# Last stage of a hybrid decoder step: small token tile first, every second sum on TensorE, four result buffers

## The reference, cut to what matters

```python
top_w, top_i = lax.top_k(pf, TOP_K)                                    # TOP_K = 2
top_w = top_w / jnp.sum(top_w, axis=-1, keepdims=True) * p_sel[:, None]
...
act = jax.nn.silu(gate) * up * combine_w[:, sl, None]
out = out + jnp.einsum('nef,efd->nd', act, w_ed[sl])
...
x = x + _hier_moe(_rmsnorm(x, norm_ffn_w), w_rc, w_rf, w_eu, w_ed)
...
y_prompt = _rmsnorm(xp, norm_final_w)     # y = x * rsqrt(mean(x*x) + 1e-6) * w
y_sample = _rmsnorm(xs, norm_final_w)
```

## Time and profile before

| | us |
|---|---|
| median of 3 runs (lowest to highest) | 1739.56 (1738.46 to 1739.89) |
| the profiled execution, own time | 1737.92 |
| its span in the profile | 1736.2 |
| PE busy, whole span | 1519.3 (88%) |
| DVE busy, whole span | 700.4 (40%) |
| ACT busy, whole span | 397.1 (23%) |
| POOL busy, whole span | 222.0 (13%) |

### The profile page before, as it was taken

How to read it: one execution, slowest core, us unless ns; L and a number is a source line. 1 busy time by engine, 2 the same in 40 slices (tenths; PEclk the granted TensorE clock), 3 DMA queues, 4 the chain that set the end, 5 groups by cost and what they waited for, 6 DMA issues and landing times. The chain is left out here.

```text
span 1736.2 us, 16020 instructions
## 1 busy us (share of the span) xinstructions
PE 1519.3 (88%) x6054; PEld 947.5 (55%) x6054; DVE 700.4 (40%) x1086; ACT 397.1 (23%) x639; POOL 222.0 (13%) x224
## 2 busy tenths in 40 slices
PE   8889999989998989699999599999807999999970
PEld 6556666645655656356989366555403444444430
DVE  4378676023243322885785333221241111111118
ACT  4111101015565563131211500011101111111113
POOL 0000010000000000254287000000041000000004
PEclk9998999999999999799899899999958999999995
DMA  5261148411100113324101722111127999999938
GB/s 160 72 101 49 50 131 240 116 50 40 38 27 26 38 26 89 92 62 139 57 1 29 298 75 75 62 60 64 43 73 302 377 367 373 370 368 367 368 144 292
DMA packets 191315, 247.83 MB, mean 143 GB/s; under 512 B 62548, under 2 KB 125432, under 8 KB 190976
## 3 DMA queue, kind: packets, MB, share of 16 engines
q1 hardware_dynamic: 165508, 186.79, 33.7%
q10 hardware_dynamic: 18140, 34.48, 5.1%
q0 software_dynamic: 7584, 25.44, 3.9%
HBM read 188.86 MB, written 57.82 MB: 142 GB/s over the span
## 5 line engine op out<-in xcount | busy, mean ns | idle before, releaser
L654 PE MATMUL P<-arena 128*128 128x352 f32 (+1 forms) x1728 | 547.0, 473 | 5.2 <-ACT arena L1791 5.2
L654 PEld LDWEIGHTS P<-arena 128*128 128x128 f32 (+1 forms) x1728 | 329.4, 194 | 193.1 <-issue 37.4
L1083 PE MATMUL P<-arena 128*128 128x512 f32 x512 | 227.8, 598 | 0.8 <-ACT arena L2060 0.8
L1083 PEld LDWEIGHTS P<-arena 128*128 128x128 f32 x512 | 95.8, 192 | 110.0 <-issue 110.0
L1031 PE MATMUL P<-arena 128*128 128x512 f32 (+1 forms) x288 | 126.8, 594 | 1.9 <-DVEq L1532 1.9
L999 PE MATMUL P<-arena 128*128 128x352 f32 x384 | 115.4, 464 | 10.1 <-DVE arena L1518 10.1
L1070 PE MATMUL P<-arena 128*128 128x512 f32 x256 | 115.3, 593 | 0.9 <-DVE arena L1661 0.9
L1641 DVE COPY arena<-P 128x512 f32<-128x512 f32 x32 | 22.1, 692 | 213.7 <-PE P L1057 213.7
L999 PEld LDWEIGHTS P<-arena 128*128 128x128 f32 x384 | 73.7, 192 | 52.0 <-issue 12.1
L1031 PEld LDWEIGHTS P<-arena 128*128 128x128 f32 (+1 forms) x288 | 50.9, 181 | 66.7 <-issue 64.2
L579 POOL TENSOR_TENSOR arena<-arena,N 64x256 f32<-64x256 f32 x96 | 80.0, 833 | 49.7 <-ACT arena L1994 26.9
(11 more groups left out here) (384 smaller groups left out, 1842.4 us busy)
## 6 DMA issues: line engine op xcount, KB each, us to landing
arena<-in_w_expert_up_dram SPq DMA_DIRECT2D x32, 2048.0 KB, 12.2
arena<-in_w_expert_down_dram SPq DMA_DIRECT2D x32, 1024.0 KB, 8.2
arena<-in_w_in_dram SPq DMA_DIRECT2D x36, 512.0 KB, 3.8
y_d<-arena ACTq DMA_DIRECT2D x32, 512.0 KB, 7.7
gate_d<-arena ACTq DMA_DIRECT2D x16, 528.0 KB, 4.1
arena<-gate_d SPq DMA_DIRECT2D x16, 528.0 KB, 4.5
arena<-in_x_prompt_dram SPq DMA_DIRECT2D x16, 512.0 KB, 4.3
y_d<-zero SPq DMA_DIRECT2D x1, 8192.0 KB, 33.2
```

Of the source, the lines that this page charges most:

```text
L654: m = pe.matmul(P[0:p, b + j, 0:TBK], w[:, k, 0:p], hT[:, k, TBK * j:TBK * j + TBK], start=f, stop=l)
L1083: m = pe.matmul(P[:, i % 2, :], xgT[i % 2][:, k, :], WU[i % NWE][:, k, :], start=k == 0, stop=k == KD - 1)
```

## The change

The order of the token tiles in the tail becomes `ORDER` = tile 8 (32 rows), then 0, 1, ..., 7; p counts the place in this order. At odd p (tiles 0, 2, 4, 6) PE makes the sum in two banks of PSUM of its own: `x1` through `ident`, then the two gathered tiles through diagonal matrices `DG` of the weights, six `pe.matmul` of 512 columns a tile, of which the two of `x1` stand ahead of the wait for the gathers. At even p (tiles 8, 1, 3, 5, 7) DVE sums as before. DVE scales all nine tiles; its order becomes C0, N0, C2, N1, N2, C4, N3, N4, C6, N5, N6, C8, N7, N8. There are four `yout` buffers and four store semaphores (two of them reused). The eight `DG` matrices are built by DVE while it works on expert tile 6.

```diff
-        yout = [at(q + 6432 + i * D, D) for i in range(2)]
+        yout = [at(q + 4384 + i * D, D) for i in range(4)]
+        DG = h2T[0]
...
+        s_out4 = s_yst + [s_wo, s_wf]
+        STORED = (0, 0, 16, 16)
...
+        ORDER = [TT_ - 1] + list(range(TT_ - 1))
+
+        def summed_by_pe(p):
+            return p % 2 == 1
+
+        def bank_sum(p):
+            return P[:, 2 * (p // 2):2 * (p // 2) + 2, :]
...
 @block.gpsimd
-            for i in range(TT_):
+            for p, i in enumerate(ORDER):
                 n = rows(i)
-                if i >= 3:
-                    pool.wait_ge(s_acc, i - 2)
+                if p >= 3 and summed_by_pe(p - 3):
+                    pool.wait_ge(s_job, N_JOBS + (p - 3) // 2 + 1)
+                elif p >= 3:
+                    pool.wait_ge(s_acc, (p - 3) // 2 + 1)
                 for j in range(2):
                     pool.indirect_dma_start(yg[2 * i + j][0:n], None, y_d,
                                             bass.IndirectOffsetOnAxis(pos_i[0:n, j, i:i + 1], 0)
-                                            ).then_inc(s_yg[i % 3], 16)
+                                            ).then_inc(s_yg[p % 3], 16)
...
 @block.tensor
                 down(hi - 1)
+                pe.wait_ge(s_yoa, hi)
+                pe.wait_ge(s_yov, hi)
 
             pe.wait_ge(s_te, 1)
             expert_tiles(pe, run)
+
+            pe.wait_ge(s_mix, 2)
+            for p, i in enumerate(ORDER):
+                if not summed_by_pe(p):
+                    continue
+                for o in range(2):
+                    pe.matmul(bank_sum(p)[:, o, :], ident, x1[:, i, 512 * o:512 * o + 512], start=True, stop=False)
+                pe.wait_ge(s_yg[p % 3], 32 * (p // 3 + 1))
+                for j in range(2):
+                    for o in range(2):
+                        m = pe.matmul(bank_sum(p)[:, o, :], DG[:, 2 * (p // 2) + j, :], yg[2 * i + j][:, 512 * o:512 * o + 512],
+                                      start=False, stop=j == 1)
+                m.then_inc(s_job, 1)
...
 @block.vector
                     dve.tensor_tensor(hact[i % 2], gact[i % 2], P[:, i % 2, FF:2 * FF], ALU.mult).then_inc(s_ha, 1)
+                    if i == 6:
+                        for p in range(1, TT_, 2):
+                            for j in range(2):
+                                m = dve.tensor_scalar(DG[:, 2 * (p // 2) + j, :], ident, w12[j][:, ORDER[p]:ORDER[p] + 1], None,
+                                                      ALU.mult)
+                        m.then_inc(s_mix, 1)
...
-            def combine(i):
+            def combine(p):
+                i = ORDER[p]
                 n = rows(i)
-                dve.wait_ge(s_yg[i % 3], 32 * (i // 3 + 1))
+                dve.wait_ge(s_yg[p % 3], 32 * (p // 3 + 1))
...
-            combine(0)
-            for i in range(TT_):
+            def normed(p):
+                i = ORDER[p]
                 n = rows(i)
-                a = 4 * (i % 2)
-                o = x1[0:n, i, :]
-                if i + 1 < TT_:
-                    combine(i + 1)
-                dve.wait_ge(s_sqf, 2 * (i + 1))
+                a = 4 * (p % 2)
+                dve.wait_ge(s_sqf, 2 * (p + 1))
                 link(dve.reciprocal(st[0:n, a + 3:a + 4], st[0:n, a + 2:a + 3]))
-                if i >= 2:
-                    dve.wait_ge(s_yst[i % 2], 16 * (i // 2))
-                dve.scalar_tensor_tensor(yout[i % 2][0:n], o, st[0:n, a + 3:a + 4], WF[0:n, :], ALU.mult,
+                if p >= 4:
+                    dve.wait_ge(s_out4[p % 4], STORED[p % 4] + 16 * (p // 4))
+                o = bank_sum(p).rearrange("p a b -> p (a b)") if summed_by_pe(p) else x1[0:n, i, :]
+                dve.scalar_tensor_tensor(yout[p % 4][0:n], o, st[0:n, a + 3:a + 4], WF[0:n, :], ALU.mult,
                                          ALU.mult).then_inc(s_yout, 1)
+
+            for p in range(0, TT_, 2):
+                combine(p)
+                if p > 0:
+                    normed(p - 1)
+                normed(p)
...
 @block.scalar
-            for i in range(TT_):
+            for p, i in enumerate(ORDER):
                 n = rows(i)
-                a = 4 * (i % 2)
-                act.wait_ge(s_acc, i + 1)
-                if i >= 2:
-                    act.wait_ge(s_yout, i - 1)
-                act.activation(JF[0:n, :], x1[0:n, i, :], ACT.Square, accum_out=st[0:n, a:a + 1]).then_inc(s_sqf, 1)
-                act.wait_ge(s_sqf, 2 * i + 1)
+                a = 4 * (p % 2)
+                if summed_by_pe(p):
+                    act.wait_ge(s_job, N_JOBS + p // 2 + 1)
+                    o = bank_sum(p).rearrange("p a b -> p (a b)")
+                else:
+                    act.wait_ge(s_acc, p // 2 + 1)
+                    o = x1[0:n, i, :]
+                if p >= 2:
+                    act.wait_ge(s_yout, p - 1)
+                act.activation(JF[0:n, :], o, ACT.Square, accum_out=st[0:n, a:a + 1]).then_inc(s_sqf, 1)
...
 @block.sync
-            for i in range(TT_):
-                sp.wait_ge(s_yout, i + 1)
+            for p, i in enumerate(ORDER):
+                sp.wait_ge(s_yout, p + 1)
                 dst = y_p[0, 128 * i:128 * i + 128, :] if i < 8 else y_s.rearrange("b t d -> (b t) d")
-                sp.dma_start(dst, yout[i % 2][0:rows(i), :]).then_inc(s_yst[i % 2], 16)
+                sp.dma_start(dst, yout[p % 4][0:rows(i), :]).then_inc(s_out4[p % 4], 16)
```

More of the change, by code:

```diff
@@ L2088, in _ @@
             expert_tiles(act, run)
-            for i in range(TT_):
+            for p, i in enumerate(ORDER):
                 n = rows(i)
-                a = 4 * (i % 2)
-                act.wait_ge(s_acc, i + 1)
-                if i >= 2:
-                    act.wait_ge(s_yout, i - 1)
-                act.activation(JF[0:n, :], x1[0:n, i, :], ACT.Square, accum_out=st[0:n, a:a + 1]).then_inc(s_sqf, 1)
-                act.wait_ge(s_sqf, 2 * i + 1)
+                a = 4 * (p % 2)
[8 more added lines that the diff above has]
+                act.activation(JF[0:n, :], o, ACT.Square, accum_out=st[0:n, a:a + 1]).then_inc(s_sqf, 1)
+                act.wait_ge(s_sqf, 2 * p + 1)
                 act.activation(st[0:n, a + 2:a + 3], st[0:n, a:a + 1], ACT.Sqrt, scale=1.0 / D,
@@ L2319, in _ @@
             expert_tiles(sp, run)
-            for i in range(TT_):
-                sp.wait_ge(s_yout, i + 1)
+            for p, i in enumerate(ORDER):
+                sp.wait_ge(s_yout, p + 1)
                 dst = y_p[0, 128 * i:128 * i + 128, :] if i < 8 else y_s.rearrange("b t d -> (b t) d")
-                sp.dma_start(dst, yout[i % 2][0:rows(i), :]).then_inc(s_yst[i % 2], 16)
-            for b in range(2):
-                sp.wait_ge(s_yst[b], 16 * ((TT_ + 1 - b) // 2))
+                sp.dma_start(dst, yout[p % 4][0:rows(i), :]).then_inc(s_out4[p % 4], 16)
+            for b in range(4):
+                sp.wait_ge(s_out4[b], STORED[b] + 16 * ((TT_ + 3 - b) // 4))
             for sm in s_cvo:
```

## The result

The kernel after takes 1740.99 us, the median of 20 runs (1737.87 to 1744.01); the kernel before, run beside it, takes 1738.47 us (20 runs, 1737.09 to 1742.42). The ratio is 1.0014, 95% interval 1.0007 to 1.0020: 2.5 us slower, small but clear of the noise. The forecast was 1738.9 us, 0.7 us faster, with 0.58 on no change beyond 0.2%. The time lies inside the range, but the sign is wrong. The bound of 0.2% was also too coarse: with 20 runs a side, 0.07% can be told here.

The account below looks back on a forecast made before the run. DVE and the transfers were taken as near-bounds of the tail; 3.5 us less after the last full gather's landing, against 2.8 us later landing, gave -0.7 us and 1738.9 us, range 1734.5 to 1744.0.

Parts of the forecast that it names:

- The two near-bounds: In the tail, DVE at 3.9 us a tile and the transfers at 4.2 us a full tile, both nearly binding.
- The p=0 start: Head of the tail: the 32-row tile's gathers land at 1695.7, 1.1 us earlier than DVE's start before.
- The price of TensorE's calls: Sums on PE: 0.88 us a float32 call, so 3.5 us for the four calls behind the gathers at full clock.
- The scaling from PSUM: DVE's scaling of PE-made sums, read from PSUM, was costed the same as before.
- the eight `DG` builds: On DVE during an expert tile: 2.3 us of work once, taken as costing nothing because DVE is idle there.
- the cold start of p=1: TensorE's first tail sum starts at 1699.3, runs 6 us at half clock, and ends at 1705.9.
- the term "p=8", "I take 1726.8": Last pair of gathers: released by the p=5 sum at 1719.3, landing between 1725.9 and 1727.3, taken as 1726.8.
- side case: One clock drop at the p=5 sum while PE waits for gathers: 1.5 us more, giving 1740.4.
- the hole: The gather of p=4 waits for TensorE's sum of p=1, so the transfer queue is empty for about 3 us.
- The full tile at the end: A full tile now comes last; its store was priced at 2.6 us against 1.9 for the small one.
- Rival 1: PE sums release gathers in time and transfers keep pace: -3.5 us, 1736.1, at best 1734.5; chance 0.35.
- Rival 2: TensorE stays at 1.2 GHz in its four sums: +8.2 us, 1747.8; chance, partly or wholly beyond +3.5 us, 0.20.

Follow-up runs that it names:

- e1: The kernel after with four filler matmuls on TensorE between the identity calls of p=5 and the wait for its gathers; 1.0023 of the kernel before.
- e10: e1 with four more filler matmuls in front of the identity calls of p=7; 1.0011 of the kernel before.
- e15: The kernel after with each gather released by the sum of p-2 instead of p-3; 1.0105 of the kernel before.
- e5: The kernel after with gathers released by the sum of p-4 instead of p-3; 0.9985 of the kernel before.
- e2: The kernel after with a semaphore per token tile, so POOL issues all 18 gathers without waiting for a sum; 0.9977 of the kernel before.
- e6: The kernel after with the tiles in their old order, 0 to 8, the small one last; 1.0001 of the kernel before.
- e14: The same edit as e6, the kernel after with the old tile order, run on another chip; 1.0001 of the kernel before.
- e13: The kernel after with every sum back on VectorE, keeping small tile first, four buffers and release by p-3; 1.0014 of the kernel before.
- e7: e2 (all gathers issued without a wait) with the tiles in their old order; 0.9981 of the kernel before.
- e4: The kernel before with one edit, the 32-row tile first in the tail; 1.0002 of the kernel before.

## Why the prediction was wrong, step by step

**Right.** The two near-bounds, and that the change frees one of them only. The p=0 start: VectorE at 1694.8 (1695.7 forecast), a stall of 2.82 us before N0. The price of TensorE's calls: eight rows take 3.70 us at the full clock (3.5 forecast). The table in the Trainium skill (VectorE: DVE Perf Modes, the errata section) would have given a quarter of it; for float32 calls this trace does not agree with it. The scaling from PSUM took 1.284 us, as costed. No cost of the eight `DG` builds shows: the tail begins 0.3 us earlier than before. From the last landing to the end of the span 8.7 us (forecast 8.7).

**Wrong without harm: the cold start of p=1.** The forecast let the sum of p=1 start at 1699.3 at the half clock and end at 1705.9. TensorE began its two identity calls only at 1694.75 and ended them at 1698.53, as the gathers landed. The granted clock was 0.50 during these calls and 0.84 from 1698.40 to 1702.60, and the sum took 4.33 us. The release of p=4 came at 1703.0, 2.9 us early, and those of p=6 and 7 at 1709.5 and 1713.8 (forecast 1711.2, 1715.1). This lead was used up by transfers that took longer than the forecast's 6.55 us (p=4: 7.9 us from release to landing) and by the slow sum of p=5.

**Wrong: the term "p=8", "I take 1726.8".** Release 1721.6 instead of 1719.3, landing 1729.4 instead of 1726.8. These 2.6 us are the whole difference between -0.7 and the profile's +1.9. In this profile 2.3 of the 2.6 us are in the release: the sum of p=5 was costed at the full clock, 3.7 us, and took 6.26. The prediction had one such drop as a side case, +1.5 us and 1740.4, close to the measured 1741.0. That nearness is luck, because the runs do not bear out its reason: with the clock held (e1, e10) the release came earlier and the time stayed (1.0023, 1.0011). What the runs show in its place is how much is in flight when a sum holds the next gather: e15 is 16 us slower than the kernel after, e5 and e2 are 5 and 6.4 us faster by their ratios, in the directions that a running-dry queue gives. I had seen the hole ("the queue runs dry for about 3 us") and priced it once, at p=4, and had not carried it to p=8, where the full tile stands last.

**Wrong: the full tile at the end.** I gave the full tile at the end only its longer store (2.6 us instead of 1.9), and took its own transfer behind the p=5 sum as one more tile. By e6 and e14 the order is worth 2.3 us in this kernel and nothing in the kernel before.

**The rivals.** Rival 1 (the transfers keep their pace, 1736.1) is what e2 then made true by another road, with 4 us instead of 3.5. Rival 2 (half clock) was right in the row and wrong in the effect: the other three sums took 3.7 to 4.3 us.

**Open.** e13 measured the frame as slow with VectorE's sums; how its cost splits between the stalls for the root, the release and the small tile at the head was not taken apart. That the gathers' release and the tile order are what the change lost by is shown by taking each away; by which transfer the 2.5 us arise is only read from single profiles. Why e1 is above e10, when e10 has the same edit and more, is not explained; their intervals overlap from 1.0014 to 1.0020.

## What to carry to other kernels

Work moved off a busy engine pays only if the new engine does not hold a release: before offloading a step, look up who waits for its semaphore, here the next gather, and let one more transfer be in flight (or drop the wait, where buffers allow) first. Where only three tiles may be in flight, a small one takes a whole place, and a full-sized one last stands behind the slowest release (e6, e14: 2.3 us). A price for a hole in the transfers belongs at each place where it recurs, the last one above all.

## What the runs showed of the hardware

TensorE began its first instruction of the tail 12.62 us after its last one before it, with the releaser given as issue; the evictions that it waits for start at 1682.17 and take 0.69 us. POOL, which stands behind the same branches and could pass them only once the last results had landed at about 1688, issued its first gather 5.2 us before that. The prediction had taken these calls as long done by 1699.3. In this profile no time is seen to hang on it, since the gathers of p=1 land only at 1698.4. What it spends the time on was not tested.

The granted clock fell after short pauses (0.59 from 1713.00 to 1721.30 in the kernel after, 1.00 from 1705.50 to 1709.20), but not by their length alone. After 2.57, 1.35 and 0.24 us without work the sum took 3.70 us (e7, e10), after 3.3 to 3.5 us 5.40 (e1, e2, e5, e7), after 4.11 us 6.26 (the kernel after); but also 5.40 after 5.08 us (e14), 5.55 after 5.84 and 6.54 after 5.04 us (e15).

A gather issue of POOL took 0.95 us by itself. Where a VectorE `scalar_tensor_tensor` with both large inputs in SBUF had been running for 0.11 us or more, the issue ended some 0.82 us after that instruction (0.73 to 0.84 in 86 rows of 15 traces), and so took up to 1.9 us: 1.93 at 1722.62 in e1 beside the sum from 1722.45 to 1723.73, 1.35 at 1706.78 in the kernel after, 1.94 at 1702.78 in the kernel before. Two rows are longer, 3.12 us (e4) and 2.68 us (e5); there the next VectorE instruction had begun before the first one ended, and the issue ended 0.81 us after that next one. Beside a scaling that reads PSUM the issue stayed at 0.94 us (1713.79 in the kernel after, 0.16 us behind the scaling's start), and also behind a start only 0.01 to 0.07 us earlier (1703.03 in the kernel after). The 16 DMA engines moved 410 GB/s from 1709.80 to 1719.80 and 420 from 1719.80 to 1723.70 in e2, with gathers and stores mixed, above the 370 that I had taken as the rate of a full queue.
